# LN2's gains turned by PE in the first expert's up stage, place 21 loaded after LN1, and the first tokens gathered by column sets

## The reference

```python
h = layer_norm(ALPHA * h + mix, ln1_g, ln1_b)
h = layer_norm(ALPHA * h + memory_cross_attention(h, mem_n, ...), ln2_g, ln2_b)
logits = h @ w_router + b_router                  # 32 experts, top 4, softmax of the four
for e in range(32):
    hid = clamped_swiglu(h @ w_mlp1[e] + b_mlp1[e])          # 1024 -> 2048 -> 1024
    y = y + combine[:, e:e + 1] * (hid @ w_mlp2[e] + b_mlp2[e])
h = layer_norm(ALPHA * h + y, ln3_g, ln3_b)
```

## Time and profile before

| what | value |
|---|---|
| median of 3 runs | 1135.61 us (1135.2 to 1135.63) |
| the profiled execution | 1137.09 us, its span 1135.2 us |
| PE, DVE, ACT busy | 96%, 28%, 20% of the span |
| bytes by DMA | 446.74 MB, mean 394 GB/s |
| chain that ended last | PE 58%, DMA 35% |

### The profile page before, as it was taken

One profiled execution on the slowest core, in us unless ns is written; L12 is line 12 of the kernel. 1 busy time (PEld: TensorE's weight loads), 2 busy tenths in 40 slices (PEclk: granted clock), 3 DMA queues, 4 the chain that ended last, 5 costly groups with the idle time before them and its releaser, 6 DMA issues.

```text
span 1135.2 us, 15726 instructions
## 1 busy us (share of the span) xinstructions
PE 1084.9 (96%) x6536; PEld 522.0 (46%) x6536; DVE 322.2 (28%) x733; ACT 228.6 (20%) x411; POOL 8.1 (1%) x14
## 2 busy tenths in 40 slices
PE   9999999989999999999999999999999999999996
PEld 6888899843333333343333333333333333334331
DVE  6987775581111111121111111111111111012112
ACT  5667565440000100010010000000000000001001
POOL 0000000000000000000000000000000000000000
PEclk9999999999999999999999999999999999999999
DMA  9866868699999999999999999999999999999996
GB/s 354 295 193 238 289 209 331 230 388 419 436 431 435 432 433 432 435 433 433 432 434 434 432 435 433 433 432 435 433 432 433 434 434 431 431 430 429 432 426 250
DMA packets 41728, 446.74 MB, mean 394 GB/s; under 512 B 4832, under 2 KB 5728, under 8 KB 25088
## 3 DMA queue, kind: packets, MB, share of 16 engines
q1 hardware_dynamic: 41408, 445.76, 94.0%
q10 hardware_dynamic: 288, 0.52, 0.1%
HBM read 445.22 MB, written 1.05 MB: 393 GB/s over the span
## 4 chain that ended last, share of the span: by engine, by line
PE 58%; DMA 35%; SPq 3%; DVE 3%; issue 1%; ACT 0%; DVEq 0%
DMA ring<-in_w_mlp 33%; PE bank L1155 23%; PE bank L1199 9%; PE bank L685 5%; PE bank L687 5%; PE bank L686 5%; PE bank L1057 4%; PE bank L1045 2%; DMA w_raw<-in_w_in 2%; SPq L609 1%; PE bank L1094 1%; SPq L488 1%; SPq L502 1%; PE bank L927 1%; PE bank L911 1%; PE bank L1113 1%
## 5 line engine op out<-in xcount | busy, mean ns | idle before, releaser
L1155 PE MATMUL bank<-ring,live 128*64 128x512 f32 x2048 | 468.2, 605 | 27.9 <-DMA ring<-in_w_mlp 27.7
L1155 PEld LDWEIGHTS bank<-ring,live 128*64 128x64 f32 x2048 | 143.8, 138 | 310.4 <-issue 286.0
L1199 PE MATMUL bank<-ring,live 128*64 128x512 f32 x992 | 220.8, 596 | 6.8 <-DMA ring<-in_w_mlp 6.8
L1919 DVE COPY live<-bank 128x256 f32<-128x256 f32 x32 | 13.6, 425 | 527.8 <-PE bank L1087 527.8
L1199 PEld LDWEIGHTS bank<-ring,live 128*64 128x64 f32 x992 | 70.8, 137 | 130.8 <-issue 122.6
L1517 ACT ACTIVATE live<-bank 128x512 f32<-128x512 f32 x31 | 18.5, 597 | 325.1 <-PE bank L1094 325.1
L1589 DVE TENSOR_TENSOR w_low<-w_raw,w_high 128x1024 fp32r<-128x1024 f32 x61 | 72.3, 1221 | 23.8 <-ACT w_high L1291 23.6
L2009 DVE TENSOR_SCALAR live<-bank 128x256 f32<-128x256 f32 x64 | 24.2, 420 | 193.1 <-PE bank L1155 193.1
L1291 ACT ACTIVATE w_high<-w_raw 128x1024 fp32r<-128x1024 f32 x61 | 63.1, 1059 | 34.7 <-PE bank L687 16.6
L1513 ACT ACTIVATE live<-live 128x512 f32<-128x512 f32 x32 | 20.3, 635 | 239.4 <-DVE live L2009 239.4
L1045 PEld LDWEIGHTS bank<-pick,live 128*128 128x128 bf16 x1488 | 52.0, 118 | 27.0 <-issue 27.0
(11 more groups left out here) (253 smaller groups left out, 859.2 us busy)
## 6 DMA issues: line engine op xcount, KB each, us to landing
ring<-in_w_mlp SPq DMA_DIRECT2D x73, 4096.0 KB, 47.1
ring<-in_w_mlp SPq DMA_DIRECT2D x34, 2048.0 KB, 49.2
ring<-in_w_mlp SPq DMA_DIRECT2D x22, 1024.0 KB, 11.0
w_raw<-in_w_in SPq DMA_DIRECT2D x21, 512.0 KB, 10.0
w_raw<-in_w_mem_kv SPq DMA_DIRECT2D x16, 512.0 KB, 4.9
w_raw<-in_w_mix_out SPq DMA_DIRECT2D x8, 512.0 KB, 5.4
w_raw<-in_w_mem_q SPq DMA_DIRECT2D x8, 512.0 KB, 3.9
w_raw<-in_w_mem_o SPq DMA_DIRECT2D x8, 512.0 KB, 6.0
```

The source lines that it names most:

```text
L1155: mm = pe.matmul(up[j][64 * g:64 * g + SLOTS, :], x_e[:, k, :], columns(row, j, g), start=False, stop=(k == KC - 1))
L1199: mm = pe.matmul(to[64 * g:64 * g + SLOTS, :], stationary[:, P * c + 64 * u:P * c + 64 * u + SLOTS], slot(at)[:, col:col + 512], start=(u ...
```

## The change

**Gains.** LN2's gain and bias are no longer loaded into `gb`. PE makes them from `token_cols`, which has them by columns: `turn_gains(part, q)` transposes four of these columns, each broadcast over 128, into a bank, so that all 128 partitions hold 512 values of the gain (part 0) or the bias (part 1). It does this after each of the steps k = 0 to 3 of the first up stage. DVE's `normalise` becomes `scale_tokens` (four, by q and then t) and `shift_tokens` (four, by t and then q); they read the bank, with neighbouring columns 128 values apart, and wait for `gains_turned`.

**Place 21.** As `gb` is free once LN1 is through, SP loads place 21 where it loaded LN2's gains (at unit 56), not behind the first loads of expert 2.

**Gather by column sets.** `gather_first(t, i)` now takes columns 4m and 4m + 1 for i = 0, and 4m + 2 and 4m + 3 for i = 1. So the copy of bank 3 alone gives the first two transposes; `turn_first(0)` makes them, and `turn_first(1)` the other two after the first half of step k = 0.

**Bias ahead.** The first expert's bias products (`add_up_bias`) are issued ahead of `gather_first`.

**First place in halves.** The first 1 MB of expert 2 goes in two transfers, the first issued after half of step k = 0.

**Constant products.** `KEPT_BUSY` has 4, 4 and 5 in three waits in place of 12 in one.

```diff
-KEPT_BUSY = {"first picks": 12}
+KEPT_BUSY = {"second sums": 4, "first bias": 4, "second ranks": 5}
...
-        turn_banks = [banks[3], banks[7], banks[4], banks[5]]
+        gain_banks = [[banks[2], banks[6]], [banks[4], banks[5]]]
+        turn_banks = [banks[3], banks[4], banks[7], banks[5]]
...
                 elif place == 21:
-                    sp.wait_ge(ln_ready, 12)
+                    sp.wait_ge(ln_ready, 8)
...
                 if u == 56:
-                    sp.wait_ge(ln_ready, 8)
-                    load_gains(a["ln2_g"], a["ln2_b"])
+                    prefetch(21, 1)
...
-            for quarter, used, landed in ((0, first_used, parts_in[0]), (1, up_used, first_half_in[0]),
-                                          (2, first_used, parts_in[1]), (3, up_used, piece_in[0])):
-                sp.wait_ge(used, quarter // 2 + 1)
-                part = slice(2048 * quarter, 2048 * (quarter + 1))
+            for eighths, used, count, landed in (((0, 1), first_used, 1, parts_in[0]), ((1, 2), first_used, 2, parts_in[0]),
+                                                 ((2, 4), up_used, 1, first_half_in[0]), ((4, 6), first_used, 3, parts_in[1]),
+                                                 ((6, 8), up_used, 2, piece_in[0])):
+                sp.wait_ge(used, count)
+                part = slice(1024 * eighths[0], 1024 * eighths[1])
                 sp.dma_start(slot(0)[:, part], expert_src(2, 0)[:, part]).then_inc(landed, 16)
-            prefetch(21, 1)
...
+            def turn_gains(part, q):
+                if part == 0 and q == 0:
+                    pe.wait_ge(token_cols_in, 16)
+                    pe.wait_ge(drained[2], bank_jobs[2])
+                    pe.wait_ge(drained[6], bank_jobs[6])
+                elif part == 1 and q == 0:
+                    pe.wait_ge(x_odd, KC // 2)
+                    pe.wait_ge(x_e_ready, 1)
+                for i in range(4):
+                    c = 4 * q + i
+                    mm = pe.transpose(gain_banks[part][q][:, P * i:P * (i + 1)],
+                                      token_cols[:, part, c:c + 1].broadcast_to([P, P]), ident)
+                mm.then_inc(gains_turned, 1)
...
-                    at = 512 * q + S * i
-                    mm = pe.matmul(banks[3 + 4 * i][64 * q:64 * q + SLOTS, 0:S], pick_first[:, t, :], h2[:, t, at:at + S],
+                    pairs = h2[:, t, 512 * q:512 * (q + 1)].rearrange("p (m a n) -> p m a n", a=2, n=2)[:, :, i, :]
+                    mm = pe.matmul(banks[3 + 4 * i][64 * q:64 * q + SLOTS, 0:S], pick_first[:, t, :], pairs,
...
+                        if first and k == 0 and j == 0:
+                            mm.then_inc(first_used, 1)
+                            turn_first(1)
...
+                    if first and k < 4:
+                        turn_gains(k // 2, k % 2)
...
+            def columns_of(t, q):
+                return h2[:, t, 512 * q:512 * (q + 1)].rearrange("p (m i) -> p m i", i=4)
+            def gain_rows(part, q):
+                dve.wait_ge(gains_turned, 2 * part + q + 1)
+                return gain_banks[part][q][:, :].rearrange("p (i m) -> p m i", i=4)
+            def scale_tokens(t, q):
+                x = columns_of(t, q)
+                step(dve.scalar_tensor_tensor(out=x, in0=x, scalar=ln_s[:, 4 + t, 1:2], in1=gain_rows(0, q),
                                               op0=ALU.mult, op1=ALU.mult))
+            def shift_tokens(t, q):
+                x = columns_of(t, q)
+                dve.tensor_tensor(x, x, gain_rows(1, q), ALU.add).then_inc(ln_ready, 1)
...
-            dve.wait_ge(gb_in, 96)
+            for q in range(2):
+                for t in range(NT):
+                    scale_tokens(t, q)
             for t in range(NT):
                 for q in range(2):
-                    normalise(t, q)
+                    shift_tokens(t, q)
```

More of the change, by code:

```diff
@@ L968, in logits @@
                 if t:
+                    keep_busy("second sums")
                     wait_drained(pe, "rT", 1, 1)
@@ L978, in keep_busy, with turn_first @@
                     pe.matmul(banks[4][:, 0:P], ident_b[:, :], ident_b[:, :], start=True, stop=True)
+            def turn_gains(part, q):
[11 more added lines that the diff above has]
+                mm.then_inc(gains_turned, 1)
             def gather_first(t, i):
                 for q in range(2):
-                    at = 512 * q + S * i
-                    mm = pe.matmul(banks[3 + 4 * i][64 * q:64 * q + SLOTS, 0:S], pick_first[:, t, :], h2[:, t, at:at + S],
+                    pairs = h2[:, t, 512 * q:512 * (q + 1)].rearrange("p (m a n) -> p m a n", a=2, n=2)[:, :, i, :]
+                    mm = pe.matmul(banks[3 + 4 * i][64 * q:64 * q + SLOTS, 0:S], pick_first[:, t, :], pairs,
                                    start=(t == 0), stop=(t == 1))
                 return mm
[L988 to L995, removed]
+            def turn_first(half):
+                for i in range(2 * half, 2 * half + 2):
+                    if i % 2 == 0:
+                        pe.wait_ge(first_high_half if half else first_low_half, 1)
+                    else:
+                        bank_for(pe, "Y", 0, i // 2)
+                    pe.transpose(turn_banks[i][:, 0:P], first_rows[:, S * (i // 2) + i % 2:S * (i // 2 + 1):2], ident)\
                         .then_inc(gathered if i == 3 else turned_first, 1)
@@ L1003, in between, with columns, add_up_bias @@
                     turn_sums(0, 1)
+            up = banks[0:2]
+            def columns(rows, j, g):
+                return rows[:, 1024 * j:1024 * (j + 1)].rearrange("p (m a n) -> p m a n", a=2, n=8)[:, :, g, :]
+            def add_up_bias(n, first=False):
+                pe.wait_ge(hot_ready, n)
+                pe.wait_ge(up_read, n)
+                for j in range(2):
+                    for g in range(2):
+                        mm = pe.matmul(up[j][64 * g:64 * g + SLOTS, :], hot[:, :], columns(bias_parts, j, g),
+                                       start=True, stop=False)
+                        if first and j == 0 and g == 0:
+                            mm.then_inc(turned, 1)
+                mm.then_inc(hot_used, 1)
             project_rows(15, left_o, (("mo", 1, 0), ("mo", 1, 1)), by_tile=True, between=between)
@@ L1012, in _ @@
             pe.matmul(b[:, 0:E], tri_b[:, :], mask_b[:, 0, :], start=True, stop=True).then_inc(filled_by("rank", 0), 1)
-            keep_busy("first picks")
+            keep_busy("first bias")
+            for i in range(2):
+                pe.wait_ge(drained[i], bank_jobs[i])
+            add_up_bias(1, first=True)
             pe.wait_ge(drained[3], bank_jobs[3])
@@ L1019, in _ @@
             gather_first(0, 0)
+            keep_busy("second ranks")
             b = bank_for(pe, "rank", 1)
@@ L1031, in _ @@
                 gather_first(1, i).then_inc(first_summed, 1)
-            up, ty, xg = banks[0:2], banks[2], banks[3]
+            ty, xg = banks[2], banks[3]
             acc = [[banks[4 + 2 * t + g] for g in range(2)] for t in range(NT)]
-            for i in range(2):
-                pe.wait_ge(drained[i], bank_jobs[i])
             def gather():
@@ L1095, in turn_hidden @@
                 mm.then_inc(hid_turned, 1)
-            def columns(rows, j, g):
-                return rows[:, 1024 * j:1024 * (j + 1)].rearrange("p (m a n) -> p m a n", a=2, n=8)[:, :, g, :]
             def wait_early(half):
@@ L1105, in up_stage @@
                          tokens=False, scatter_first=False, early=False, quarters_in=None, seventh=None):
-                pe.wait_ge(hot_ready, n)
-                pe.wait_ge(up_read, n)
-                for j in range(2):
-                    for g in range(2):
-                        mm = pe.matmul(up[j][64 * g:64 * g + SLOTS, :], hot[:, :], columns(bias_parts, j, g),
-                                       start=True, stop=False)
-                        if first and j == 0 and g == 0:
-                            mm.then_inc(turned, 1)
-                mm.then_inc(hot_used, 1)
+                if not first:
+                    add_up_bias(n)
                 def scatter_two_ago():
@@ L1126, in up_stage @@
                 if first:
-                    turn_first()
+                    turn_first(0)
                 else:
```

10 lines of the change are left out of this document (3 added, 7 removed).

## The result

The change is slower: 1141.49 us median of six runs (1141.09 to 1142.68), beside 1135.27 us for the kernel before on the same chip (1134.98 to 1135.63). The ratio is 1.0057, interval 1.0044 to 1.0070, so 6.2 us, well beyond the 0.2% that can be told. The forecast was 1137.0 us within 1131.6 to 1139.8 us; the measured time lies above that range, on the side of the third rival but not by its mechanism. The profiled execution took 1141.47 us, its span 1139.7; it lies at the median, while the one shown of before lay 1.8 us above its own.

What follows compares the result with a forecast made beforehand. The weight stream was taken to set the end. Fewer bytes (2.4 us) and the dip (up to 1.7) are used up by PE's 6.7 us delay: +0.7 + 0.7 = +1.4, 1138.5 profiled, 1137.0 us median, range 1131.6 to 1139.8.

Steps and rivals of the forecast that it cites:

- the third rival: DVE's reads of turned gains from PSUM, 512 bytes between neighbours, are slow: 1139.6 us; chance 0.15.
- The dip: Stream at 239 to 245 us lost 1.7 us; issuing the first place in halves can win back 0 to 1.7 us.
- the bytes: LN2's two gain loads go, so the stream later carries 1024 KB less: 2.4 us gained.
- it lands at 285.5 + 2.46 + 9.69 = 297.6. That is 0.7 us later than before: First 4096 KB load, issued when the first down stage is done, meets an empty queue and lands 0.7 us late.
- late engines: Instruction loads delay single DMA engines, no longer hidden when the stream restarts: 0 to 1.5 us, taken as 0.7.
- Behind it PE gains on the stream again (...), and nothing runs dry: After the first 4096 KB load: an expert takes PE 26.0 us, its weights 29.1 us, so no further hole.
- The median of the runs, 1135.61, lies 1.5 us under that execution: Conversion from the 1138.5 us forecast for a profiled execution to the predicted median of 1137.0 us.
- The stream did not stay full: Rival: gather late by less than 1.9 us, 4.1 us kept, 1131.5 us; full or nearly so, chance 0.2.
- The clock's 1.5 us: After PE's 4.6 us wait at the gather, the granted clock falls to 1.2 GHz: 0 to 3.4 us, taken as 1.5.
- Slow reads of PSUM: The third rival: DVE's eight scales and shifts take twice their time, PE 9.3 us late, 1139.6 us; chance 0.15.

Runs made afterwards that it cites:

- e3: Kernel before with eight or four more DVE operations ahead of LN2's normalising: 1142.29 us with eight, 1138.46 us with four.
- e2: The change with both gains turned behind step k = 0 and both biases behind k = 1: 1136.59 us.
- e7: Kernel before with place 21 early and LN2's gains turned by PE in place of twelve constant products, biases behind k = 0: 1133.80 us.
- e10: The kernel of e7 once more, in more rounds: 1133.56 us, ratio 0.9983 to the kernel before.
- e8: The kernel before, unchanged, run again for a second profile: one execution of 1136.14 us.
- e5: The change with place 21 loaded behind the first loads of expert 2, as before: 1141.30 us.
- e4: The change with 70 constant products on PE between the first up stage and the first gather: 1139.72 us.
- e11: The change without two groups of constants, gains turned ahead of the bias and biases behind k = 1: 1135.41 us, ratio 1.0001 to before.
- e9: The change with the 4 MB load issued at 286.0 split in halves, the first issued after half the first down stage: 1139.96 us.
- e1: The change with LN2's gains loaded and normalised by DVE, and place 21 loaded, as before: 1136.76 us, ratio 1.0007.

## Why the prediction was wrong

**PE and DVE: right.** Predicted and measured: start of the up stage 236.0 and 235.80; last gains turned 245.7 and 246.2; last shift ended 247.8 and 248.1; gather 257.3 and 257.66; idle PE 4.6 and 4.39 us; lost to the clock 1.5 and 1.64 us; the 4 MB load issued 285.5 and 286.00. The delay of PE was 6.7 in the forecast and 7.2 us in the trace. Pairs of columns as moving operand were taken as free, and nearly were (twelve passes in 1.61 us, 1.57 before). e3 shows that such a delay alone makes the result, e2, e7 and e10 that the gains can be turned without it.

**The dip and the bytes: spent, as forecast, and with a hole not foreseen.** The halves won back 0.3 of 1.7 us (364 GB/s for 348), which is no more than two executions of before differ by (348, and 362 in e8). With place 21's load gone from behind the quarters, and the load behind them issued at 249.87 and not 246.91, the stream ran low at 245 to 256 us (1.4 us). e5, which has the megabyte back in that place and loses less there, takes the same time, so the hole costs nothing of its own.

**The step that failed** is "it lands at 285.5 + 2.46 + 9.69 = 297.6. That is 0.7 us later than before". The 297.6 are issue, fixed part and bytes, and the fixed 2.46 us came from a load whose engines ended only 0.58 us apart (214.73 to 215.31). This was held against 296.9, the end on the slowest engine of an execution whose engines were 3.56 us apart. On the first engine the same load of before ended at 293.33. Like with like, the forecast said 297.6 - 0.6 - 293.3 = 3.7 us late; measured 297.50 - 293.33 = 4.2, as the issue came 0.5 us later than forecast. So the number for after was near, and the number that it was compared with was not. Counted on the slowest engines, the load landed 2.3 us late (299.20 and 296.89) where 0.7, and 0.7 more for late engines, were forecast. The same reading later put the end of the queue at 287.2 instead of 283.7 into the plan of e3, 3.5 us of allowance that nothing had; e3's half dose showed that.

**"Behind it PE gains on the stream again (...), and nothing runs dry" failed too.** The next load is issued 9.52 us after this one, and this one's bytes take 9.66: it came 2.0 us ahead of the queue's end, and a hole of 1.0 us followed. 4.2 + 1.0 is the 5.2 us by which that load ends later on the first engine (308.14 - 302.98).

**The median.** "The median of the runs, 1135.61, lies 1.5 us under that execution" was carried over to the change. Before's profiled execution was a late one: e8, the same kernel, landed the load issued at 288.3 us 0.94 us earlier and took 0.95 us less. The change's profiled execution lay at its median, so this subtraction was 1.5 us too much. With the predicted 1138.5 for a profiled execution and the measured 1141.47, the error splits into 3.0 us of stream and 1.5 us of conversion. Of the 6.2 us between the medians 5.2 are accounted for on the first engine (5.6 against e8); the rest is left open, as is the 0.7 us that the forecast gave to late engines: the last engine lags by 0.7 to 3.4 us where the stream had holes and by 2.0 to 3.6 us where it had next to none.

**The rivals.** The stream did not stay full. The clock's 1.5 us were priced well: e4 got 1.3 to 2.4 us back. Slow reads of PSUM are refuted: with 512 bytes between neighbours a scale took 1.53 / 2 = 0.77 us and a shift 0.69 or 1.88 / 3 = 0.63, as before from SBUF (0.74, 0.69). The Trainium skill, "SBUF — State Buffer", section "Door 1: The DMA port swizzle", says that PSUM patterns that are not contiguous slow matmuls significantly; for these reads by DVE no run here shows a cost.

## What to carry to other kernels

A landing is the end on the slowest of 16 engines; before you say that a load comes later or that a queue lasts until then, compare the same engine in both, or look at a second profile. Ask of each issue that an engine's delay moves how far ahead of the queue's end it still comes: here 2.5 us or more was free for the loads of 4 MB, nearly every such issue that came later left a hole, the one behind it too, and some loads of 2 MB lost a little even at 3 us. Work that another engine reads (a turned gain) belongs into a wait ahead of the stage or behind its first step, not one group behind each of its steps: with the same sixteen transposes the whole change was 6 us slower than before in one place and level with it in the other (e11), and without the rest of the change 2 us faster (e7, e10).

## What was not expected of the hardware

*A restart has two parts.* The load of 265.44 met empty engines. Windows of after:

```profile
264.40:265.40 1.00, 1.00 (x7) 0.19 (x4) 0.00 (x0) 0.00 (x0) 0.00 (x0) 1.00 0.00 0
265.40:266.40 1.00, 1.00 (x6) 0.38 (x8) 0.00 (x0) 0.37 (x1) 0.00 (x0) 1.00 0.08 16
...
267.50:268.00 0.50, 0.50 (x6) 0.21 (x4) 0.00 (x0) 0.00 (x0) 0.00 (x0) 1.00 1.03 426
```

The first packets of 16 KB start at 266.40, 0.96 us after the issue (0.95 to 0.96 in e4, e5 and e9 too), and take 0.9 to 1.5 us where later ones take 0.61; full speed comes at 267.5, 2.1 us after the issue. The Trainium skill, "DMA: Bandwidth & Descriptors", section "Anatomy of one DMA — SWDGE (gpsimd) path", puts most of a fixed 2 us behind the last byte, for DMAs that GpSimd issues. Here SP issues, and 2.1 us lie ahead of the full rate. Some bytes flow in the later part of them, so a stream that restarts loses less, by estimate 1.6 us from the issue on (0.96 us, and 0.6 us that each engine's first packet takes longer).

*Holes ahead of a queue that is not yet empty.* A load issued 1.9 to 2.4 us ahead of the first engine's end still left 0.2 to 1.6 us of hole in seven of eight cases (the second hole of e2, both e3, e4, e5, e11 and after; 0.1 us in e1's first). Issued 2.5 us ahead or more (both in before, e7, e8 and e10, the second in e1), none did. This is for the two loads of 4 MB. The second of the four 2 MB loads, whose bytes take 4.84 us, left 0.2 to 0.5 us of hole in five kernels where it was issued 2.9 to 3.2 us ahead (e2, both e3, e5, e11) and 0.1 us or less in three at 2.9 (e4, e9, after). Why the hole varies so was not found.

*The clock.* After waits of PE of 0.4 to 1.8 us the gather took 1.74 to 1.76 us (before, e2, e4, e7, e10, e11); after 2.9 to 7.6 us it took 2.3 to 2.7. What was lost up to the turned weights (line 1071 of before) did not grow with the wait: 1.0 us after 2.90 (e1) and after 4.67 (e3, four), 1.3 us after 7.58 (e3, eight), and after the same wait of 4.4 us 1.1 us (e9), 1.6 us (the change) and 2.0 us (e5).
